# Four gated slots, gates and additions split by tile, and part of a modulation on TensorE between mixers and FFNs

## The chip, the cores and the metric

One core of one Trainium2 chip. The time is that of one launch in device microseconds, the median of several runs.

## What is computed

Two blocks of two layers each over one sequence of 256 tokens and width 1024, all in float32. In the first block every sublayer is a sandwich: the input is normed, scaled and shifted by a modulation of `c`; the output is normed again, gated and added.

```
def sandwich(x, mod, g_pre, g_post, fn):
    shift, scale, gate = mod
    h = rms_norm(x, g_pre) * (1.0 + scale[:, None]) + shift[:, None]
    return x + gate[:, None] * rms_norm(fn(h), g_post)
```

`mod` is `silu(c) @ ada_w + ada_b`, split in three. Sublayers in order: hybrid mixer (pool and a gated recurrence), SwiGLU (ffn0), dilated attention (qkv, att_out), SwiGLU (ffn1). The second block has plain pre-norms: mixer (even_in, even_out), MLP, axial attention (odd_in, odd_out), MLP.

## The kernel before

Everything is held as two tiles of 128 tokens in `x[:, tt, :]`. Weights come in loads of 1 MB through six raw slots (SyncE's queue); each load is two halves, and of every half ScalarE makes a high part (`whi`, line 513) and VectorE the low part (`wlo`, line 1210). TensorE multiplies high by high, high by low and low by high (`three`), so a product is three matmuls. Four halves of `whi` and `wlo` exist, and a split waits until TensorE is done with the half four before. TensorE's program order is written out by hand; engines meet by counting semaphores only.

Between two sublayers lies a seam, numbered j = 1 to 7 (line 2118 `turn(j)`). At seams 1 to 4 the output of the sublayer stands in four PSUM banks, `ps[:, 4 + i, :]`, i = 0 to 3: tile `i // 2`, half `i % 2` of the columns. What happens there:

- ScalarE, `norms(j)` (line 590): squares of y by bank with a running sum (`square_y`), the root of each tile (`root_y`, Ln and Exp), squares of the new x (`square_x`) and their roots (`root_x`).
- VectorE, `renew(j, bank)` (line 1327): y times gate (`gate_y`, line 1303) into `xn_of(p)[1]`, which has two slots of 512 columns, so the third and the fourth gate wait for the additions that read the first two; the addition to x once the root is there (`update_x`, line 1311); the small sums ahead of a root (`mean_y`, `mean_x`); x times its root (`scaled_x`, line 1324), tile 0 in one piece, tile 1 in two; and between them `mod_cols` (lines 1256 to 1258), which waits for `cols_sum` and makes the scale and shift columns out of PSUM.
- TensorE: column sums over partitions of a modulation (`sum_cols`, 16 matmuls with one column), dummies (`keep_warm`, into a bank that nobody reads), 16 transposes of the scaled x (`turn`, line 2126).
- then `pre(j)`: ScalarE and VectorE turn each of the eight transposed chunks k into a shifted float32 copy, a high part `hhi` and a low part `hlo` (line 1371); TensorE's first product of the next layer waits for `hlo` of each k (`turned_in`). With 2 x 128 output columns per half (`up`), a chunk k is worth 6 matmuls.

The modulation itself is worked out on VectorE beside other work: `ada_item` (lines 1220, 1223) multiplies one of eight chunks of a block of `ada_w` (512 columns) by a column of silu(c) and adds to `acc_a` or `acc_b`; Pool's queue loads the halves of a block (`ada_blocks`, line 439), each when `ada_step` says that the half in the same slot is used. Gate rows are summed over partitions by matmuls of `ones` (`sum_gates`), then `gate_add` and `gate_gain` on VectorE (lines 1267, 1273). The blocks 6 to 13 are worked out inside ffn0.

## Time and profile before

| what | us |
|---|---|
| median of 3 runs (1340.04 to 1345.56) | 1343.15 |
| the profiled execution, own time | 1342.11 |
| its span | 1340.2 |
| TensorE busy, share of the span | 1324.5, 99% |
| VectorE busy | 870.3, 65% |
| ScalarE busy | 721.7, 54% |
| mean granted clock of TensorE | 0.991 |

In the profile, engines are PE (TensorE), PEld (its weight loads), DVE (VectorE), ACT (ScalarE), POOL and SP (the queues). A busy TensorE may be at work on dummies or at half clock, so its share alone does not tell what a seam costs. Matmuls of float32 operands are two records each, transposes one.

### The profile page before, as it was taken

What the parts mean: (1) busy time and instruction counts of PE and PEld (TensorE: products, weight loads), DVE (VectorE), ACT (ScalarE), POOL (GpSimd) and SP (SyncE); (2) the same over time, 40 slices, a digit from 0 to 9 for tenths busy, and PEclk for the clock granted to TensorE, in tenths of its full rate; (3) what the DMA queues carried; (4) which work ended last, traced back from release to release, by engine and by line L of the source; (5) the groups of instructions that cost most, each with busy time, mean ns of one, the idle gap of its engine ahead of it and who ended that gap; (6) DMA issues with size and microseconds to landing.
All of it is one profiled execution on the core that took longest, in us unless ns stands there. A gap on an engine that the chain in (4) does not pass through costs nothing.

```text
span 1340.2 us, 22440 instructions
## 1 busy us (share of the span) xinstructions
PE 1324.5 (99%) x8876; PEld 1197.7 (89%) x8876; DVE 870.3 (65%) x1140; ACT 721.7 (54%) x1070; POOL 49.9 (4%) x76
## 2 busy tenths in 40 slices
PE   8999999999999999999999999999999999999999
PEld 7998899999899779999999899889999888899997
DVE  6889888885898566555565675565555577655554
ACT  3666644444644556444466763555555666655553
POOL 0100000000111000000001000000000000000000
PEclk8999999999899999999999999999999999999999
DMA  9978789985699624555537444455555552355540
GB/s 353 388 267 278 268 282 316 311 297 185 234 358 353 198 59 146 188 186 187 188 140 232 155 140 144 129 169 191 188 190 188 171 168 95 126 189 189 188 156 32
DMA packets 147362, 275.54 MB, mean 206 GB/s; under 512 B 4728, under 2 KB 85392, under 8 KB 147161
## 3 DMA queue, kind: packets, MB, share of 16 engines
q1 hardware_dynamic: 132176, 220.21, 48.7%
q0 software_dynamic: 13872, 52.05, 11.5%
q10 hardware_dynamic: 1240, 2.26, 0.5%
q8 instruction: 51, 0.84, 0.3%
q14 instruction: 23, 0.18, 0.0%
HBM read 273.40 MB, written 1.10 MB: 205 GB/s over the span
## 4 chain that ended last, share of the span: by engine, by line
PE 86%; DVE 6%; DMA 4%; issue 2%; ACT 2%; SPq 0%; ACTq 0%; DVEq 0%
PE ps L1985 84%; DMA raw<-in_ada_w 2%; DMA ada_ring<-in_ada_w 2%; DVE acc_a L1223 2%; DVE wlo L1210 1%; PE ps L2126 1%; PE ps L2362 1%; DMA raw<-in_hyb_w_in 1%; ACT whi L513 0%; ACT xn L567 0%; DVE xn L1324 0%; PE ps L2470 0%; ACT small L574 0%; DVE x L1318 0%; PE ps L2663 0%
## 5 line engine op out<-in xcount | busy, mean ns | idle before, releaser
L1210 DVE TENSOR_TENSOR wlo<-raw,whi 128x1024 fp32r<-128x1024 f32 x400 | 485.5, 1224 | 356.0 <-ACT whi L513 354.5
L513 ACT CAST whi<-raw 128x1024 fp32r<-128x1024 f32 x400 | 417.6, 1051 | 472.8 <-PE ps L1985 456.7
L1985 PE MATMUL ps<-hhi,whi 128*128 128x256 f32 x1792 | 507.4, 283 | 2.9 <-DVE hlo L1371 2.4
L1985 PE MATMUL ps<-hhi,wlo 128*128 128x256 f32 x1792 | 500.7, 279 | 0.0
L1985 PE MATMUL ps<-hlo,whi 128*128 128x256 f32 x1792 | 499.9, 279 | 0.0
L1985 PEld LDWEIGHTS ps<-hhi,whi 128*128 128x128 f32 x1792 | 335.9, 187 | 9.1 <-issue 6.2
L1985 PEld LDWEIGHTS ps<-hlo,whi 128*128 128x128 f32 x1792 | 336.2, 188 | 4.7 <-issue 2.4
L1985 PEld LDWEIGHTS ps<-hhi,wlo 128*128 128x128 f32 x1792 | 336.5, 188 | 0.0
L1985 PE MATMUL ps<-whi,hidhi 128*128 128x512 f32 x432 | 170.3, 394 | 0.0
L1985 PE MATMUL ps<-wlo,hidhi 128*128 128x512 f32 x432 | 169.1, 392 | 0.0
L1985 PE MATMUL ps<-whi,hidlo 128*128 128x512 f32 x432 | 168.6, 390 | 0.0
L1985 PE MATMUL ps<-whi,hhi 128*128 128x512 f32 (+1 forms) x256 | 101.8, 398 | 2.0 <-ACT att1o L790 0.8
L1223 DVE SCALAR_TENSOR_TENSOR acc_a<-ada_ring,sc,acc_a 128x512 f32<-128x512 f32 (+1 forms) x126 | 94.7, 752 | 6.8 <-DMA ada_ring<-in_ada_w 2.6
L1985 PEld LDWEIGHTS ps<-whi,hidlo 128*128 128x128 f32 x432 | 81.1, 188 | 18.6
L1985 PE MATMUL ps<-wlo,hhi 128*128 128x512 f32 (+1 forms) x256 | 97.6, 381 | 0.0
L1985 PE MATMUL ps<-whi,hlo 128*128 128x512 f32 (+1 forms) x256 | 97.5, 381 | 0.0
L1985 PEld LDWEIGHTS ps<-whi,hidhi 128*128 128x128 f32 x432 | 81.1, 188 | 16.0 <-issue 0.2
L1985 PEld LDWEIGHTS ps<-wlo,hidhi 128*128 128x128 f32 x432 | 81.1, 188 | 15.4 <-issue 0.2
L1985 PEld LDWEIGHTS ps<-whi,hhi 128*128 128x128 f32 x256 | 48.3, 189 | 14.5 <-issue 3.9
L1985 PEld LDWEIGHTS ps<-wlo,hhi 128*128 128x128 f32 x256 | 48.2, 188 | 10.4 <-issue 1.4
L1985 PEld LDWEIGHTS ps<-whi,hlo 128*128 128x128 f32 x256 | 48.2, 188 | 10.3
L439 POOL DMA_DIRECT2D ada_ring<-in_ada_w x40 | 30.4, 760 | 307.9 <-DVE acc_a L1223 222.1
(238 smaller groups left out, 1156.6 us busy)
## 6 DMA issues: line engine op xcount, KB each, us to landing
raw<-in_ffn_w_in SPq DMA_DIRECT2D x44, 1024.0 KB, 6.4
ada_ring<-in_ada_w POOLq DMA_DIRECT2D x40, 1024.0 KB, 7.3
raw<-in_w_mlp_up SPq DMA_DIRECT2D x32, 1024.0 KB, 5.4
raw<-in_w_mlp_down SPq DMA_DIRECT2D x32, 1024.0 KB, 5.0
raw<-in_ffn_w_out SPq DMA_DIRECT2D x22, 1024.0 KB, 5.0
raw<-in_att_w_qkv SPq DMA_DIRECT2D x18, 1024.0 KB, 6.8
raw<-in_w_in_even SPq DMA_DIRECT2D x18, 1024.0 KB, 4.9
raw<-in_hyb_w_in SPq DMA_DIRECT2D x10, 1024.0 KB, 12.0
```

The lines of the kernel that those rows point to most:

```text
L439: pool.dma_start(ada_ring[:, kh, :, :], src).then_inc(ada_in[kh], 16)
L513: A.copy(whi[:, H % 4, :], raw[:, slot(n), h * HALF:(h + 1) * HALF]).then_inc(s["hi_ready"], 1)
L1210: V.tensor_tensor(wlo[:, H % 4, :], raw[:, slot(n), h * HALF:(h + 1) * HALF], whi[:, H % 4, :].bitcast(F32), ALU.subtract).then_inc(s["lo_ ...
L1223: ins = V.scalar_tensor_tensor(out=out, in0=ada_ring[:, kh, kk, :], scalar=sc[:, k:k + 1], in1=out, op0=ALU.mult, op1=ALU.add)
L1985: return pe.matmul(out, lhsT, rhs, start=first, stop=last, skip_group_check=True)
L2126: m = pe.transpose(turned_ps(j, k)[:, tt * P:(tt + 1) * P], xn[:, tt, k * P:(k + 1) * P], ident[:, :])
L2362: m = pe.transpose(dl_turned(p, i)[:, (j - j0) * P:(j - j0 + 1) * P], dl_block(p, j), ident[:, :])
```

## The change

Seams 1 to 4 (`POST`), ScalarE and VectorE: y times gate goes to four slots of 512 columns, in `xn_of(p)[0]`, and the squares' discarded outputs go to `xn_of(p)[1]`. Tile 0's additions come right behind tile 0's root; each gate and addition of tile 1 follow one another. The two squares of x's tile 0 become one over 1024 columns (`square_tile`), whose sum needs no `mean_x`; `root_tile` takes it directly. The scaling of tile 0 stands behind all additions and behind `mean_x` of tile 1.

Ahead of ffn0: items 6 and 7 of block 5 leave VectorE; TensorE does them as 8 matmuls of one column each, straight from the ring into the bank of the column sums, which then add to it. After the 2nd, 6th, 10th and 14th of the 16 sums stand two dummies each, and in front of the transposes one in place of seven. VectorE's splits of halves 28 and 29 move: one behind the scaling of tile 1, one into `pre(1)` behind k = 3.

Ahead of qkv: TensorE sums the second gate ahead of the last but one down product in place of the last; VectorE's `gate_add` moves into the last body of ffn0. Ahead of ffn1: four dummies in place of seven.

```diff
--- before.py
+++ after.py
@@ -258,6 +258,11 @@
+        POST = (1, 2, 3, 4)
+        def means_x(j, tt):
+            return 2 * j + tt + 1 - sum(i in POST for i in range(j + 1))
         def xn_of(j):
@@ -557,14 +562,26 @@
                 y_ready(act, p, i)
-                A.activation(xn_of(p)[0][:, i // 2, c], ps[:, 4 + i, :], ACT.Square,
+                A.activation(xn_of(p)[1][:, i % 2, :], ps[:, 4 + i, :], ACT.Square,
                              accum_out=stat[:, i:i + 1]).then_inc(s["ssq_y"], 1)
+            def square_tile(j):
+                act.wait_ge(s["x_ready"], 4 * (j - 1) + 2)
+                A.activation(xn_of(j - 1)[1][:, :, :].rearrange("p a b -> p (a b)"), x[:, 0, :], ACT.Square,
+                             accum_out=stat[:, 5:6]).then_inc(s["ssq_x"], 2)
+            def root_tile(j):
+                act.wait_ge(s["ssq_x"], 4 * j + 2)
+                root(small[:, 5, 3:4], stat[:, 5:6], eps[:, 0:1], "ssq_x", 4 * j + 2, "root_x")
...
                 act.wait_ge(s["x_ready"], 4 * (j - 1) + i + 1) if j else act.wait_ge(s["x_in"], 16)
-                A.activation(xn_of(j)[0][:, i // 2, c], x[:, i // 2, c], ACT.Square,
+                junk = xn_of(j)[1][:, i % 2, :] if j in POST else xn_of(j)[0][:, i // 2, c]
+                A.activation(junk, x[:, i // 2, c], ACT.Square,
                              accum_out=stat[:, 4 + i:5 + i]).then_inc(s["ssq_x"], 1)
@@ -585,20 +602,24 @@
                 root(small[:, 5, 3 + tt:4 + tt], stat[:, 5 + 2 * tt:6 + 2 * tt], small[:, 5, 7 + tt:8 + tt],
-                     "mean_x", 2 * j + tt + 1, "root_x")
+                     "mean_x", means_x(j, tt), "root_x")
...
-                if j in (1, 2, 3, 4):
+                if j in POST:
                     square_y(j - 1, 0)
...
                     square_y(j - 1, 2)
-                    square_x(j, 0)
                     square_y(j - 1, 3)
                     root_y(j - 1, 1)
-                else:
-                    square_x(j, 0)
+                    square_tile(j)
+                    root_tile(j)
+                    square_x(j, 2)
+                    square_x(j, 3)
+                    root_x(j, 1)
+                    return
+                square_x(j, 0)
                 square_x(j, 1)
@@ -1298,19 +1319,17 @@
                 dve.wait_ge(s["ssq_y"], 4 * p + i + 1)
-                if i >= 2:
-                    dve.wait_ge(s["x_ready"], 4 * p + i - 1)
-                V.tensor_tensor(xn_of(p)[1][:, i % 2, :], ps[:, 4 + i, :], gg[:, p % 2, cols_of(i)], ALU.mult) \
+                V.tensor_tensor(xn_of(p)[0][:, i // 2, cols_of(i)], ps[:, 4 + i, :], gg[:, p % 2, cols_of(i)], ALU.mult) \
                     .then_inc(s["y_gated"], 1)
-            def update_x(p, tt):
+            def update_x(p, i):
+                tt = i // 2
                 dve.wait_ge(s["root_y"], 2 * p + tt + 1)
-                dve.wait_ge(s["y_gated"], 4 * p + 2 * tt + 2)
-                for i in (2 * tt, 2 * tt + 1):
-                    V.scalar_tensor_tensor(out=x[:, tt, cols_of(i)], in0=xn_of(p)[1][:, i % 2, :],
-                                           scalar=r_y[:, tt:tt + 1], in1=x[:, tt, cols_of(i)], op0=ALU.mult,
-                                           op1=ALU.add).then_inc(s["x_ready"], 1)
+                dve.wait_ge(s["y_gated"], 4 * p + i + 1)
+                V.scalar_tensor_tensor(out=x[:, tt, cols_of(i)], in0=xn_of(p)[0][:, tt, cols_of(i)],
+                                       scalar=r_y[:, tt:tt + 1], in1=x[:, tt, cols_of(i)], op0=ALU.mult,
+                                       op1=ALU.add).then_inc(s["x_ready"], 1)
@@ -1327,25 +1346,28 @@
                 p = j - 1
-                if j in (1, 2, 3, 4):
+                if j in POST:
                     dve.wait_ge(s["gates_ready"], p + 1)
                     gate_y(p, 0)
+                    mean_y(p, 0)
                     gate_y(p, 1)
-                    mean_y(p, 0)
                     update_x(p, 0)
+                    update_x(p, 1)
+                    mean_y(p, 1)
                     gate_y(p, 2)
-                    mean_y(p, 1)
+                    update_x(p, 2)
                     gate_y(p, 3)
-                    mean_x(j, 0)
-                    update_x(p, 1)
-                elif j:
+                    update_x(p, 3)
+                    mean_x(j, 1)
+                    scaled_x(j, 0, 0, D)
+                else:
                     add_y(p, 0)
...
                     add_y(p, 3)
-                scaled_x(j, 0, 0, D)
-                mean_x(j, 1)
+                    scaled_x(j, 0, 0, D)
+                    mean_x(j, 1)
                 if bank is not None:
@@ -1371,6 +1393,8 @@
                             shifted(k + 3)
+                        if j == 1 and k == 3:
+                            split(2 * FIRST["hyb_out"] + 9)
                     else:
@@ -1395,6 +1419,8 @@
                     split_some(g, it, before)
+                    if modulations and isinstance(it, int) and g == NG1 - 1:
+                        gate_add(1, 2)
                     dve.wait_ge(s["hhid_hi"], G + g + 1 + 2 * it)
@@ -1551,14 +1577,14 @@
             split(2 * FIRST["hyb_out"] + 7)
-            ada_part(acc_a, 5, 512 * 5, 1)
+            for k in (4, 5):
+                ada_item(acc_a, 5, 512 * 5, k)
             mod_gate(0, 2)
-            for q in range(4, 6):
-                split(2 * FIRST["hyb_out"] + 4 + q)
             renew(1, 0)
+            split(2 * FIRST["hyb_out"] + 8)
             pre(1)
             swiglu(FIRST["ffn0"], 0, True)
-            mod_gate(1, 2)
+            gate_gain(1)
             renew(2, 3)
@@ -2098,10 +2124,12 @@
-            def sum_cols(acc, n, bank):
+            def sum_cols(acc, n, bank, first=True):
                 for i in range(16):
-                    m = mm(ps[:, bank, i:i + 1], acc[:, n + i * P:n + (i + 1) * P], ones[:, 0:1])
+                    m = mm(ps[:, bank, i:i + 1], acc[:, n + i * P:n + (i + 1) * P], ones[:, 0:1], first, True)
+                    if not first and i % 4 == 1:
+                        keep_warm(2, 1)
                 m.then_inc(s["cols_sum"], 1)
@@ -2131,13 +2159,17 @@
-                def body(g, it=0, first=False):
+                def body(g, it=0, first=False, sums=False):
...
                     up(H0 + 6 + 6 * g, it, b + 1)
+                    if sums:
+                        pe.wait_ge(s["hid_ready"], G + g + 1)
+                        pe.wait_ge(s["ada_step"], 8 * 14)
+                        sum_gates(acc_b, 0, 2)
                     pe.wait_ge(s["hhid_lo"], G + g + 1 + 2 * it)
@@ -2145,13 +2177,12 @@
                 body(1, 0)
-                with pe.Fori(1, (NG1 - 1) // 2) as i:
+                with pe.Fori(1, (NG1 - 1) // 2 - 1) as i:
                     body(0, i)
                     body(1, i)
+                body(NG1 - 3)
+                body(NG1 - 2, sums=call == 0)
                 pe.wait_ge(s["hhid_lo"], G + NG1)
-                if call == 0:
-                    pe.wait_ge(s["ada_step"], 8 * 14)
-                    sum_gates(acc_b, 0, 2)
                 last_down(H0 + 6 * NG1 - 2, hid_c(hidhi1, (NG1 - 1) % 2), hid_c(hidlo1, (NG1 - 1) % 2))
@@ -2308,9 +2339,16 @@
             out_proj("hyb_out", 2, hhi[:, 4:8, :], hlo[:, 4:8, :], 2, False, True)
-            pe.wait_ge(s["ada_step"], 8 * 6)
-            sum_cols(acc_a, 2 * 512, 0)
-            turn(1, 7)
+            pe.wait_ge(ada_in[1], 16 * 6)
+            for k in (6, 7):
+                if k == 6:
+                    pe.wait_ge(s["ada_step"], 8 * 6 - 2)
+                for i in range(4):
+                    m = mm(ps[:, 0, 12 + i:13 + i], ada_ring[:, 1, k - 4, i * P:(i + 1) * P], sc[:, k:k + 1],
+                           k == 6 and i == 0, False)
+                m.then_inc(s["ada_step"], 1)
+            sum_cols(acc_a, 2 * 512, 0, False)
+            turn(1, 1)
             swiglu(FIRST["ffn0"], 0, 1)
@@ -2421,7 +2459,7 @@
             sum_cols(acc_a, 0, 0)
-            turn(3, 7)
+            turn(3, 4)
             swiglu(FIRST["ffn1"], 1, 3)

```

## Rows read from the trace of the kernel before

**Rows 1.** Page, part 1: busy us, share of the span, instructions.

```profile
PE 1324.5 (99%) x8876; PEld 1197.7 (89%) x8876; DVE 870.3 (65%) x1140; ACT 721.7 (54%) x1070; POOL 49.9 (4%) x76
```

**Rows 2.** The chain that ended last: start us, us, what.

```profile
154.84 192.61 PE ps L1985 x1358
...
699.60 30.86 PE ps L1985 x246
```

**Rows 3.** Timeline, first seam, all engines: start, us, engine, line, out<-in, count, [idle].

```profile
141.80 2.35 DVE L1210 TENSOR_TENSOR wlo<-raw,whi 128x1024 fp32r<-128x1024 f32 x2
...
143.28 3.64 PE L1985 MATMUL ps<-ones,acc_a 128*128 128x1 f32 x32
...
144.32 0.37 SPq L366 DMA_DIRECT2D raw<-in_ffn_w_in  x1
...
146.78 3.33 PE L1985 MATMUL ps<-ident 128*128 128x128 f32 x14
...
151.03 0.16 DVE L1256 TENSOR_TENSOR shcol<-ps,cols 128x8 f32<-128x8 f32 x1
...
151.11 2.55 PE L2126 MATMUL ps<-ident,xn 128*128 128x128 f32 x16 [1.00 <-DVE xn L1324]
...
151.85 0.88 DVE L1324 TENSOR_SCALAR xn<-x,small 128x256 f32<-128x256 f32 x2 [0.38 <-ACT small L576]
...
153.21 0.56 ACT L620 ACTIVATE h<-ps,shcol,scol 128x256 f32<-128x256 f32 x1 [1.47 <-PE ps L2126]
...
156.28 0.85 DVE L1371 TENSOR_TENSOR hlo<-h,hhi 128x256 fp32r<-128x256 f32 x2
```

**Rows 4.** Stretches: length, busy (count) by engine, granted clock (PEclk), DMA share, GB/s.

```profile
30.70:34.10 3.40, 3.40 (x32) 3.40 (x32) 1.12 (x4) 1.04 (x1) 1.65 (x2) 1.00 1.05 386
34.10:37.50 3.40, 3.40 (x15) 3.17 (x15) 3.09 (x6) 2.70 (x5) 0.00 (x0) 0.50 1.05 391
143.28:146.75 3.47, 3.47 (x33) 3.47 (x32) 2.81 (x6) 1.07 (x4) 0.00 (x0) 1.00 1.03 387
146.75:150.20 3.45, 3.36 (x16) 3.06 (x15) 3.37 (x8) 3.16 (x11) 0.00 (x0) 0.51 1.04 378
344.70:348.10 3.40, 3.40 (x12) 2.21 (x12) 2.96 (x9) 2.64 (x10) 1.28 (x2) 0.50 0.16 58
348.10:351.50 3.40, 3.40 (x14) 2.89 (x14) 1.47 (x4) 1.60 (x4) 0.77 (x1) 0.50 0.88 266
351.50:352.00 0.50, 0.50 (x3) 0.25 (x2) 0.50 (x2) 0.50 (x2) 0.00 (x0) 0.94 0.99 385
501.70:505.10 3.40, 3.40 (x18) 3.20 (x17) 2.90 (x9) 2.22 (x8) 0.00 (x0) 0.51 0.00 0
```

**Rows 5.** Timeline, second seam.

```profile
345.39 2.05 PE L1985 MATMUL ps<-acc_a,ones 128*128 128x512 f32 x2
...
346.05 0.75 DVE L1324 TENSOR_SCALAR xn<-x,small 128x1024 f32<-128x1024 f32 x1
...
347.24 3.62 PE L2126 MATMUL ps<-ident,xn 128*128 128x128 f32 x16
```

**Rows 6.** Timeline, third seam.

```profile
500.90 2.58 PE L1985 MATMUL ps<-ident 128*128 128x128 f32 x14
...
503.39 2.81 PE L2126 MATMUL ps<-ident,xn 128*128 128x128 f32 x16
```

**Rows 7.** Timeline, fourth seam.

```profile
692.39 4.40 PE L1985 MATMUL ps<-ident 128*128 128x128 f32 x38
...
693.39 0.58 ACT L560 ACTIVATE xn<-ps 128x512 f32<-128x512 f32 x1
...
697.02 2.47 PE L2126 MATMUL ps<-ident,xn 128*128 128x128 f32 x16 [0.23 <-DVE xn L1324]
```

**Rows 8.** Timeline of Pool and of VectorE in ffn0.

```profile
139.78 0.75 POOL L439 DMA_DIRECT2D ada_ring<-in_ada_w  x1 [4.54 <-DVE acc_a L1223]
...
180.00 3.11 DVE L1223 SCALAR_TENSOR_TENSOR acc_b<-ada_ring,sc,acc_b 128x512 f32<-128x512 f32 x4
```

## Prediction, made before the change was run

> **What bounds the kernel now.** The page first: TensorE is busy for 99% of the span [rows 1]. So the only time that an edit between two layers can win is the time in which TensorE waits or does work that is no product of the reference, and whatever it adds to TensorE's own stream is paid in full unless it fills such a gap. The chain that ended last shows where the gaps lie: 1358 matmuls in one piece from 154.84 us, another piece from 699.60 us, and small pieces of ScalarE and VectorE only between them [rows 2]. The change touches four of these seams: before ffn0 (about 143 to 155 us), before qkv (341 to 352), before ffn1 (497 to 507) and before even_in (692 to 700). I then read each seam in the timeline, with the granted clock beside it.
>
> First seam [rows 3]: the last product of out_proj ends at 143.28; 16 column sums follow (32 records, 3.5 us to the next start, so 0.22 us each), then 7 dummies that take 3.33 us. VectorE has scaled tile 0 only at 151.1 (TensorE idle for 1.00 us before it), the second tile at 151.85, the first shifted tile comes at 153.21 and the first product at 154.84. Here the norm decides, because VectorE is still splitting weights until 144.15. The clock beside it [rows 4]: full through the column sums, 0.51 from 146.75 to 150.20. Second seam [rows 5]: tile 0 is scaled at 346.05 + 0.75 = 346.8, but TensorE is busy with half of a gate sum until 347.44 and its transposes go on until 350.86, at a clock of 0.50 throughout [rows 4]. There TensorE's own stream decides, the norm does not. Third seam [rows 6]: dummies until about 503.2, transposes from 503.39, nearly gapless, clock 0.51 [rows 4]. Fourth [rows 7]: the transposes start at 697.02, when tile 0 is scaled, after TensorE has stood waiting for that; the norm decides.
>
> **The change, part by part.**
>
> *Own slots for gated y, new order of gates and additions, one square over tile 0.* No gate has to wait for an addition any more, so the third and fourth square of y on ScalarE come as soon as their bank is full. At the fourth seam the dummies start at 692.39, so the last bank is full at about 692.6, and its square runs at 693.39 [rows 7], 0.8 us late. From there ScalarE's order is as before (root of y, square of x's first tile, its root, two squares, the last root), except that one square of 1024 columns stands for one of 512. One of 512 takes 0.58 [rows 7]; the wide one costs between 0 and 0.58 more, I take 0.45. So the last root comes 0.8 - 0.45 = 0.35 earlier at best. Against it: the scaling of tile 0 now stands behind the additions of tile 1 and behind mean_x of tile 1, which needs the square after the wide one. Tile 0 is thus scaled when it is now, within 0.1, and the first transposed columns, which are what even_in's first product waits for, come no sooner. Gain at the fourth seam: 0 to 0.3, I take 0.1. At the second the transposes start behind the gate sum either way: 0. At the third, tile 0 is scaled when it is now, tile 1 some 0.3 sooner, but the transposes there run at half clock and end when they end now: 0.
>
> *First seam, work taken from VectorE.* Two of its modulation items and two weight splits (2.35 us [rows 3]) leave the stretch ahead of the norm. VectorE's own chain then ends some 3.5 us sooner: tile 1 could be scaled near 148.3 instead of 151.85. What is late next is TensorE. Its stream after 143.28 is now 8 single-column matmuls for the two items, 16 for the sums, 8 dummies among these and one in front of the transposes. At full clock: 24 x 0.22 + 9 x 0.23 = 7.35 us (a dummy is two records, and 38 of them took 4.40 us at full clock, so 0.23 each [rows 7]). The sums are complete at 150.4, where they are complete at 146.9 now. And VectorE waits for just that: mod_cols stands in its queue ahead of the scaling of tile 1, so both scalings of tile 1 and all after them are queued behind the column sums. From the end of that wait the present rows give the rest: mod_cols at 151.03, tile 1 at 151.85, shifted tile at 153.21, product at 154.84, so 3.8 us [rows 3], 3.95 with the hand-over. First product at 150.4 + 3.95 = 154.35: 0.5 us sooner, if the clock holds.
>
> *Does it hold?* The row shows it at 1.00 through the present sums and 0.51 from 146.75 [rows 4]. The dummies come after the tenth single-column matmul, so what TensorE does up to 146.75 is nearly what it does now: I take it that the clock falls there again. Where the start of the kernel alternates single-column matmuls with a few dummies (30.7 to 34.1) the clock was 1.00 and was 0.50 right after [rows 4], so the mixture is no proof against a fall. At 146.75 a full-clock remainder of 3.65 us is left. A low stretch of 3.4 us as at this seam now does 1.7 us of it: sums complete at 146.75 + 3.4 + 1.95 = 152.1, first product 156.05, **1.2 us later** than now. No fall is the lower end (-0.5), a stretch twice as long, as from 344.7 to 351.5 [rows 4], the upper: 146.75 + 6.8 + 0.25 = 153.8, product 157.75, +2.9. I take the middle one, nearest in place.
>
> *The moved splits.* The first of the two comes behind the scalings: ready before the first product in each case; 0. The second now stands in pre(1) after the fourth low part. The low parts of k = 3 and 4 run at 156.28 to 157.13 [rows 3]; the split (1.22 us, half of the 2.35) pushes the fifth to 158.35, usable at 158.5. TensorE reaches k = 4 after 24 matmuls; at 0.125 us each (30.86 us for 246 [rows 2]) that is 157.85. It waits 0.65 us; bounds 0 and 1.22. The rest follows without a gap. I take **+0.7**.
>
> *What else is queued.* Pool's load of the next modulation half waits for items which TensorE now makes: it goes out near 145 (143.28 + 8 x 0.22) instead of 139.78, with a gain row behind it; its data are used at 180.00 [rows 8]: 0. SyncE's load at 144.32 [rows 3] waits for the second moved split, so near 158 to 160; its slot is used by the fourth group of splits after that, about 20 us on: 0, and 5 us at worst if it is late. The gate sum ahead of ffn0's last products is moved, not removed: 0. gate_add inside the last body delays the low half of the hidden tile by 1.22 us, beside the whole down product of the group before, after which it is wanted: 0. Pulling the gates off the second seam frees VectorE there, where TensorE decides: 0.
>
> *Three dummies fewer at the third seam.* Transposes start when tile 0 is scaled, not when dummies end: 0 if the clock returns about 505, as now. Dummies and transposes stand together in that low stretch [rows 4, 6]; with fewer dummies it may return later. Half a microsecond of products at half clock costs 0.25; I take +0.2, with 2.2 as the upper end (products from 507.4 on at half clock for about 4.4 us).
>
> Whether transposes alone bring the clock back is what that rests on. The second seam shows it: from 347.24 there are only 16 transposes and one half gate sum, and the granted clock is 0.94 in the half microsecond after 351.50 [rows 4, 5]. The Trainium skill (TensorE: Matmul & The Clock Gate, "Part 4: PE-mode transpose") says that full clock does not engage for transposes, as they do not count as busy in the same way. By that rule the third seam would end on the upper value (+2.2 in place of +0.2). The trace disagrees with the rule, though not conclusively, because the gate sum stands in the same stretch.
>
> **Sum.** First seam +1.2 + 0.7, second 0, third +0.2, fourth -0.1: **+2.0 us** on the profiled execution, whose time is 1342.11 (span 1340.2 and 1.9 around it): 1344.1. The median of the three runs is 1343.15, 1.0 higher, and I forecast the change's median there: **1345.2 us**. A measurement of this kernel can tell about 0.5% from no change, 6.7 us; every case below lies within that.
>
> **The rivals.**
> - *The clock stays low for two such stretches at the first seam* (slower): +2.9 + 0.7 + 0.1 = +3.7, 1346.9. Place: the mixed column sums; price: half clock until 153.6; it decides once the dummies among single-column matmuls are too thin to bring the clock back. For it: the row at 30.7 and 34.1. Against it: 7 dummies in a row did bring it back by 150.2.
> - *The clock never falls at the first seam*: -0.5 + 0.7 + 0.1 = +0.3, 1343.4.
> - *Clock low into ffn1* (slower, place third seam): transposes do not raise it; forecast +2.0: +4.0, 1347.2. With the first rival as well +5.7, 1348.8.
> - *The norms do gain* (faster): ScalarE's earlier roots reach the first product at the third and fourth seam (-0.3 each), clock full at the first (-0.5), the fifth low part is in time (0) and the transposes of the second seam start 0.8 sooner because the clock falls later there: -1.9, 1341.3. For it: VectorE is freed of 2.35 us and more. Against: the busy TensorE rows at seams two and three.
>
> **How the numbers follow.** Forecast 0.4, longer low stretch 0.2, no fall 0.15, low into ffn1 0.1, gain 0.15. The run-to-run spread is 1340.0 to 1345.6. The range runs from below the gain case to the two slower rivals together: 1340.3 to 1349.0. Over 0.5% faster (under 1336.4) would need a gain larger than all idle time at the four seams: 0.02. Over 0.5% slower (above 1349.9) needs both slow clocks and a late load: 0.05. Within: 0.93.
>
> **What the new profile would show.** Right: a continuous TensorE stream of about 9 us from 143.3, mod_cols behind its end, transposes with no wait for scaled tiles, a wait of TensorE for the low part of about 0.7 us some 3 us into ffn0, a first product near 156. Second seam unchanged, transposes gapless. Third: 4 dummies, then a gap of over 1 us ahead of the transposes. Wrong: tile 1's scaling ahead of the column sums' end, a first product before 154, or a load that is waited for in ffn0.

## The result and the profile after

The changed kernel takes 1347.54 us (median of 12 runs, 1342.97 to 1354.02) against 1344.05 us for the kernel before (12 runs beside it, 1340.03 to 1345.75): ratio 1.0029, 95% interval 1.0015 to 1.0042, so 2 to 6 us slower. It is small, and in these runs clear of the noise; when both were run again (experiment 1) the interval was 1.0000 to 1.0031. The profiled execution has 1348.38 us. The ratios below leave out one run, of experiment 8, that took 5630.88 us.

The page of the changed kernel (span; part 1, columns as in [rows 1]) shows nothing of where the time went: TensorE is busy for 99%, as before, only longer.

```profile
span 1346.6 us, 22425 instructions
...
PE 1330.7 (99%) x8890; PEld 1204.3 (89%) x8890; DVE 868.9 (65%) x1134; ACT 721.9 (54%) x1062; POOL 49.7 (4%) x76
```

The timeline of the first seam, the lines that answer to [rows 3] (start, us, engine, line, what; L2011 is a matmul, L2154 a transpose):

```profile
146.71 1.84 PE L2011 MATMUL ps<-sc,ada_ring 128*128 128x1 f32 x16
...
148.86 0.69 PE L2011 MATMUL ps<-ident 128*128 128x128 f32 x4
149.39 0.95 PE L2011 MATMUL ps<-ones,acc_a 128*128 128x1 f32 x8
...
152.14 1.20 PE L2011 MATMUL ps<-ident 128*128 128x128 f32 x4
...
153.13 1.71 PE L2011 MATMUL ps<-ones,acc_a 128*128 128x1 f32 x8
...
156.58 0.17 DVE L1277 TENSOR_TENSOR shcol<-ps,cols 128x8 f32<-128x8 f32 x1 [5.30 <-PE ps L2011]
...
156.97 3.62 PE L2154 MATMUL ps<-ident,xn 128*128 128x128 f32 x16
157.06 0.88 DVE L1343 TENSOR_SCALAR xn<-x,small 128x256 f32<-128x256 f32 x2
...
159.62 0.57 ACT L641 ACTIVATE h<-ps,shcol,scol 128x256 f32<-128x256 f32 x1 [7.90 <-PE ps L2154]
```

and of TensorE alone right behind it:

```profile
161.25 0.35 PE L2011 MATMUL ps<-hhi,whi 128*128 128x256 f32 x1 [0.66 <-DVE hlo L1393]
...
164.73 0.36 PE L2011 MATMUL ps<-hhi,whi 128*128 128x256 f32 x1 [0.40 <-DVE hlo L1393]
```

TensorE starts its single-column matmuls at 146.71 and goes on without a gap until the transposes at 156.97: 10.26 us, where the kernel before has 7.83 with a wait of 1.00 in it. Matmuls overlap at their ends, so what two dummies (four records) cost is the time from their start to the start of what follows: 0.53 us at full clock (148.86 to 149.39) and 0.99 at half (152.14 to 153.13). VectorE's mod_cols (156.58) sits behind the end of the sums, and the scaling of tile 1 (157.06) behind that. The first product comes at 161.25, 14.54 us after the first sum (11.56 before). The clock in the same stretch (columns as in [rows 4]):

```profile
146.71:150.67 3.96, 3.96 (x37) 3.96 (x36) 3.10 (x8) 3.57 (x11) 1.29 (x2) 1.00 1.05 342
150.67:154.08 3.41, 3.41 (x20) 3.41 (x19) 0.61 (x1) 0.99 (x4) 0.00 (x0) 0.53 0.98 367
154.08:157.50 3.42, 3.42 (x17) 3.42 (x18) 0.85 (x5) 0.00 (x0) 0.00 (x0) 0.50 0.28 110
157.50:160.92 3.42, 3.09 (x15) 2.69 (x13) 2.36 (x4) 1.30 (x4) 0.00 (x0) 0.50 0.00 0
160.92:162.00 1.08, 0.75 (x6) 0.78 (x7) 1.08 (x4) 1.08 (x4) 0.00 (x0) 0.90 0.00 0
```

The clock is full (2.4 GHz) until about 150.9 (the mean of 0.53 in the second row is 0.2 us at full and the rest at half) and low (1.2 GHz) to about 161.1 (the mean of 0.90 in the last row), 10.2 us in one piece, through the rest of the sums, the dummies and all transposes.

The second, third and fourth seam, the lines that answer to [rows 5], [rows 6] and [rows 7]:

```profile
352.49 2.06 PE L2011 MATMUL ps<-acc_a,ones 128*128 128x512 f32 x2
...
352.96 0.74 DVE L1343 TENSOR_SCALAR xn<-x,small 128x1024 f32<-128x1024 f32 x1
...
354.34 2.58 PE L2154 MATMUL ps<-ident,xn 128*128 128x128 f32 x16
```

```profile
508.23 2.05 PE L2011 MATMUL ps<-ident 128*128 128x128 f32 x8
...
510.07 3.21 PE L2154 MATMUL ps<-ident,xn 128*128 128x128 f32 x16
```

```profile
699.56 0.60 ACT L565 ACTIVATE h<-ps 128x512 f32<-128x512 f32 x1 [0.69 <-PE ps L2011]
...
703.99 2.23 PE L2154 MATMUL ps<-ident,xn 128*128 128x128 f32 x16 [0.22 <-DVE xn L1343]
```

At the second, tile 0 is scaled at 353.70 (352.96 + 0.74) and TensorE's gate sum still ends later. At the third, four dummies come and then the transposes, without a gap. At the fourth, the last bank's square stands at 699.56, 0.2 us behind the start of the dummies (699.36); before it was 1.0 behind. The piece that starts with even_in in the chain that ended last, as in [rows 2], is of the same length:

```profile
706.37 30.88 PE ps L2011 x246
```

The seams from all profiles of the study, read from the timelines, all in us. A seam is counted from its first sum (the first single-column matmul; at the fourth seam the first dummy) to the next first product; ffn0 from its first product to the second seam's first sum; "low" is how long the clock was at half in one piece at the first seam:

| version | first sum at | seam 1 | low | ffn0 | seam 2 | seam 3 | seam 4 |
|---|---|---|---|---|---|---|---|
| before, profile 1 | 143.28 | 11.56 | 3.4 | 186.75 | 9.98 | 9.96 | 7.21 |
| before, profile 2 | 143.62 | 12.21 | 6.8 | 186.75 | 9.24 | 11.49 | 7.21 |
| before, profile 3 | 147.07 | 12.37 | 6.8 | 186.75 | 10.06 | 9.87 | 7.21 |
| changed, profile 1 | 146.71 | 14.54 | 10.2 | 187.65 | 9.19 | 10.73 | 7.01 |
| changed, profile 2 | 146.13 | 14.88 | 10.2 | 187.66 | 10.38 | 10.46 | 7.00 |
| first-seam part alone | 145.76 | 15.36 | 10.2 | 187.62 | 9.59 | 10.02 | 7.20 |
| first-seam part undone | 144.08 | 11.31 | 3.4 | 186.75 | 9.20 | 10.45 | 7.00 |
| the same, 7 dummies at seam 3 | 146.28 | 11.03 | 3.4 | 186.76 | 9.20 | 11.51 | 7.00 |
| no dummies among the sums | 146.95 | 11.23 | 6.8 | 187.63 | 9.19 | 9.91 | 7.01 |
| dummies in a row | 145.88 | 13.71 | 6.8 | 187.65 | 9.19 | 9.91 | 7.01 |
| split ahead of the low parts | 146.22 | 15.09 | 10.2 | 186.92 | 10.11 | 9.65 | 7.00 |
| mod_cols last | 145.51 | 15.36 | 10.2 | 187.65 | 9.16 | 9.51 | 7.00 |
| splits moved otherwise (experiment 9) | 146.38 | 10.03 | 3.4 | 186.99 | 9.19 | 9.85 | 7.00 |
| the same, one dummy | 147.41 | 10.40 | 6.8 | 186.76 | 9.18 | 9.46 | 7.00 |

Changed against before, first profiles: 6.4 us of span. 3.43 of them lie ahead of the first seam, up to which TensorE's program is the same; seam 1 gives +2.98, ffn0 +0.90, seam 2 -0.79, seam 3 +0.77, seam 4 -0.20, and the other stretches together the rest, -0.7.

The low clock at the first seam goes with the dummies among the sums: 10.2 us in all five profiles that have them there, 3.4 or 6.8 in all nine that have not, the kernel before included.

### The profile page after: what moved, and what is told of

It reads as the page before. It is cut to its first block, busy times and chain, and to the rows that moved or that the text cites. A ratio compares the mean times of both kernels' runs of the same rounds, so it can differ in the third digit from the quotient of the medians.

```text
span 1346.6 us, 22425 instructions
## 1 busy us (share of the span) xinstructions
PE 1330.7 (99%) x8890; PEld 1204.3 (89%) x8890; DVE 868.9 (65%) x1134; ACT 721.9 (54%) x1062; POOL 49.7 (4%) x76
## 4 chain that ended last, share of the span: by engine, by line
PE 96%; ACT 1%; DVE 1%; DMA 1%; issue 1%; ACTq 0%
PE ps L2011 94%; PE ps L2154 1%; PE ps L2400 1%; DMA voh<-in_voh 1%; ACT whi L518 0%; PE ps L2508 0%; DVE xn L1343 0%; DVE x L1337 0%; PE ps L2701 0%; DVE hlo L1393 0%; ACT xn L584 0%; ACT h L641 0%; ACT small L591 0%; DVE hlo L1943 0%; ACT hhi L643 0%
## 5 line engine op out<-in xcount | busy, mean ns | idle before, releaser
L2011 PE MATMUL ps<-hhi,whi 128*128 128x256 f32 x1792 | 507.0, 283 | 3.0 <-DVE hlo L1393 2.4
L2011 PE MATMUL ps<-hhi,wlo 128*128 128x256 f32 x1792 | 500.6, 279 | 0.0
L2011 PE MATMUL ps<-hlo,whi 128*128 128x256 f32 x1792 | 500.0, 279 | 0.0
L2011 PEld LDWEIGHTS ps<-hhi,whi 128*128 128x128 f32 x1792 | 335.9, 187 | 10.0 <-issue 7.4
L2011 PEld LDWEIGHTS ps<-hlo,whi 128*128 128x128 f32 x1792 | 336.3, 188 | 4.4 <-issue 2.2
L2011 PEld LDWEIGHTS ps<-hhi,wlo 128*128 128x128 f32 x1792 | 336.4, 188 | 0.0
L2011 PE MATMUL ps<-whi,hidhi 128*128 128x512 f32 x432 | 170.2, 394 | 0.0
L2011 PE MATMUL ps<-wlo,hidhi 128*128 128x512 f32 x432 | 169.3, 392 | 0.0
L2011 PE MATMUL ps<-whi,hidlo 128*128 128x512 f32 x432 | 168.6, 390 | 0.0
L2011 PE MATMUL ps<-whi,hhi 128*128 128x512 f32 (+1 forms) x256 | 102.1, 399 | 2.0 <-ACT att1o L811 0.8
L2011 PE MATMUL ps<-wlo,hhi 128*128 128x512 f32 (+1 forms) x256 | 97.8, 382 | 0.0
L2011 PEld LDWEIGHTS ps<-whi,hidlo 128*128 128x128 f32 x432 | 81.1, 188 | 18.6
L2011 PE MATMUL ps<-whi,hlo 128*128 128x512 f32 (+1 forms) x256 | 97.6, 381 | 0.0
L2011 PEld LDWEIGHTS ps<-whi,hidhi 128*128 128x128 f32 x432 | 81.1, 188 | 16.1 <-issue 0.2
L2011 PEld LDWEIGHTS ps<-wlo,hidhi 128*128 128x128 f32 x432 | 81.1, 188 | 15.3 <-issue 0.2
L2011 PEld LDWEIGHTS ps<-whi,hhi 128*128 128x128 f32 x256 | 48.4, 189 | 14.5 <-issue 3.9
L2011 PEld LDWEIGHTS ps<-wlo,hhi 128*128 128x128 f32 x256 | 48.4, 189 | 10.4 <-issue 1.4
L2011 PEld LDWEIGHTS ps<-whi,hlo 128*128 128x128 f32 x256 | 48.4, 189 | 10.3
```

Source lines behind the costliest of these rows:

```text
L2011: return pe.matmul(out, lhsT, rhs, start=first, stop=last, skip_group_check=True)
```

## The experiments

Unless said otherwise an edit is made to the changed kernel.

**1. The changed kernel again** (no edit).

> The changed kernel once more. Theory (the time is lost at the first seam, in TensorE's longer stream and at half clock): from the first column sum to ffn0's first product 13 to 15 us, against 11.56 in the profile of the kernel before; from there to the second seam's sums about 0.7 to 0.9 us more than 186.75; median 2 to 5 us above the kernel before. Rival (the two profiles differ mostly by what happens ahead of the first seam, 3.4 us of their 6.4, by chance of that execution): the first sum comes near 143.3 again in this profile, and the median is within 1.5 us of the kernel before.

1347.59 us (12 runs), the kernel before beside it 1344.11 (35 runs); ratio 1.0015, interval 1.0000 to 1.0031. Seam 1 is 14.88, ffn0 187.66. The first sum is at 146.13, not 143.3. The theory's numbers hold for the seam and ffn0; where the late start comes from is experiment 5.

**2. The first-seam part alone, in the kernel before, and 3. that part undone, in the changed kernel.**

```diff
-            ada_part(acc_a, 5, 512 * 5, 1)
+            for k in (4, 5):
+                ada_item(acc_a, 5, 512 * 5, k)
             mod_gate(0, 2)
-            for q in range(4, 6):
-                split(2 * FIRST["hyb_out"] + 4 + q)
             renew(1, 0)
+            split(2 * FIRST["hyb_out"] + 8)
...
-            sum_cols(acc_a, 2 * 512, 0)
-            turn(1, 7)
...
+            sum_cols(acc_a, 2 * 512, 0, False)
+            turn(1, 1)
```

(the edit of 2, cut: left out are the split inside `pre(1)`, the 8 item matmuls and the dummies inside `sum_cols`; 3 is the inverse of the whole)

> The kernel before with only that part: two modulation items on TensorE, dummies among the sums, two splits moved. Theory: first seam 13 to 15 us, median 2 to 5 us above the kernel before, as the changed kernel. Rival: within 1.5 us of the kernel before.

> The changed kernel with only the part ahead of ffn0 undone: both modulation items and both splits back on VectorE ahead of the norm, 16 sums and seven dummies on TensorE. Theory (all of the loss is in that part; the new order of gates and additions gives 0 to 0.5 us): first seam 11.3 to 11.6 us, no wait for the fifth low part, median 0 to 1 us below the kernel before. Rival (the new order of the norms, or three dummies fewer at the third seam, is what costs): median stays 2 us or more above the kernel before, third seam 10.7 us again instead of 9.96.

Alone: 1348.24 us, ratio 1.0029 (1.0013 to 1.0045), seam 1 15.36 (a little above the 13 to 15 expected), ffn0 187.62: the whole loss. Undone: 1342.45 us, ratio 0.9994 (0.9977 to 1.0012), seam 1 11.31, ffn0 186.75: no loss left. Both ran beside the same runs of the kernel before as experiment 1. The theory stands: the loss is in the first-seam part, and the new order of the norms costs nothing that these runs show. The fourth seam tells what that order gives: 7.20 with the old order (alone), 7.00 with the new one (undone).

**4. Why the stream is long: no dummies among the sums, and all nine dummies in a row behind them.**

```diff
-                    if not first and i % 4 == 1:
-                        keep_warm(2, 1)
...
-            turn(1, 1)
+            turn(1, 9)
```

(the last two lines in the second version only)

> The changed kernel without the eight dummies among the column sums. Theory (the dummies cost their own length and do not keep the clock up): the stream from the first single-column matmul to the last shrinks from 10.3 us to 6 to 7.5 us and the first product of ffn0 comes 2 to 4 us sooner than in the changed kernel (10.5 to 12.5 us after the first sum); median 2 to 3 us below the changed kernel. Rival (the dummies do hold the clock up in most executions, and their lack is paid in transposes and first products at half clock): first product 13 us or more after the first sum, median same as or above the changed kernel.

> The changed kernel with all nine dummies in a row behind the sums, none among them: the same 33 pieces of work on TensorE, in another order. Theory A (what costs most is the mixture: it does not bring the clock back, a row of dummies does): low clock for 3.4 or 6.8 us instead of 10.2, first seam 12 to 13.5 us. Theory B (the length of the stream alone counts): 14.3 us or more, as with the dummies among the sums. Either way the column sums end sooner, so VectorE makes the scale and shift columns while the dummies run.

Without them: 1345.27 us, ratio 1.0010 (0.9997 to 1.0023). That is 2.3 us below the median of the changed kernel beside it, but the intervals of the two ratios (1.0010, and 1.0015 in experiment 1) overlap widely, so the total does not settle it; the seam does, at 11.23. TensorE's timeline without them:

```profile
146.95 1.84 PE L2011 MATMUL ps<-sc,ada_ring 128*128 128x1 f32 x16
148.65 4.83 PE L2011 MATMUL ps<-ones,acc_a 128*128 128x1 f32 x32
153.34 0.78 PE L2011 MATMUL ps<-ident 128*128 128x128 f32 x2
153.91 3.62 PE L2152 MATMUL ps<-ident,xn 128*128 128x128 f32 x16
```

The transposes start after 6.96 us, not 10.26. In a row: 1344.38 us, ratio 1.0013 (0.9996 to 1.0030), seam 1 13.71, between what the two theories gave (12 to 13.5, and 14.3 or more), nearer the first:

```profile
145.88 1.84 PE L2011 MATMUL ps<-sc,ada_ring 128*128 128x1 f32 x16
147.58 5.58 PE L2011 MATMUL ps<-ones,acc_a 128*128 128x1 f32 x32
153.02 3.65 PE L2011 MATMUL ps<-ident 128*128 128x128 f32 x18
156.50 1.91 PE L2152 MATMUL ps<-ident,xn 128*128 128x128 f32 x16
159.59 0.35 PE L2011 MATMUL ps<-hhi,whi 128*128 128x256 f32 x1 [1.18 <-DVE hlo L1393]
```

The 32 records of the sums take 5.58 us, partly at half clock; from 156.50 the transposes take 1.91, so the clock is back by then, and the scale and shift columns are long made. The clock is low for 6.8 us in both versions here, 10.2 in the changed kernel.

What the mixture costs can be added up from start to start. The eight dummies among the sums occupy 3.04 us (two pairs at 0.53, two at 0.99); the 16 sums between them take 0.27 us more than without them; together 3.3, which is all of the difference between 14.54 and 11.23, as from the first transpose to the first product both need 4.3. At full clock the eight dummies would take 2.1 us, so about two thirds of these 3.3 us are their bare length and one third is half clock. In a row, nine dummies and the sums take 10.62 us up to the transposes, no less than in the changed kernel, but the clock is back for these, and 3.09 us later the first product comes. That share of the order, 0.8 us, rests on one profile; like versions spread from 14.54 to 15.36.

The two items themselves cost the seam nothing: with them on TensorE and without the eight dummies it is 11.23, with them on VectorE and seven dummies in front of the transposes 11.31 (experiment 3). What the first version here keeps of the loss is the 0.9 us in ffn0.

**5. The kernel before, profiled twice more.**

> The kernel before, profiled once more. Theory (what happens ahead of the first seam differs between executions of the same code): the first column sum starts anywhere from 143 to 147 us; first seam 11.0 to 12 us, ffn0 186.75. Rival (the shift of the start belongs to the changed kernels): 143.3 again.

> The kernel before, profiled a third time. Two profiles of it have the first column sum at 143.28 and 143.62 us, nine of other versions with the same code up to there at 144.1 to 147.4. Theory (chance of the execution): 144 to 147 us is as likely as not. Rival (the later start belongs to the changed kernels in some way): 143.0 to 143.9 a third time. First seam 11.3 to 12.3 us, third 9.9 to 11.5 as in the first two.

The first sum is at 143.62 and 147.07. (The recorded text counts nine other profiles; there were eleven.) The first 44 us of the kernel before, in its first profile and in its third:

```profile
0.00:44.00 44.00, 39.95 (x235) 33.79 (x236) 31.80 (x60) 20.14 (x40) 2.80 (x7) 0.88 1.00 361
```

```profile
0.00:44.00 44.00, 38.50 (x218) 32.75 (x219) 28.84 (x53) 17.81 (x35) 2.79 (x7) 0.77 0.98 350
```

The granted clock is 0.88 in the one and 0.77 in the other, which is that of the changed kernel's profile too (0.77). Over all fourteen profiles the first sum comes earliest where the clock was low for the shortest time in the first 60 us: at 143.28, 143.62 and 144.08 with 10.2, 10.2 and 13.7 us of half clock, at 145.5 to 147.4 with 17.1 or 20.5. TensorE's program up to there is the same in all versions, and the kernel before has both the earliest start and one of the latest; so 3.4 of the 6.4 us between the first two profiles are an accident of execution. The seams of the kernel before vary as well: 11.56 to 12.37 at the first, where seven dummies in a row were followed by a full clock after 3.4 us in the first profile and only after 6.8 in the two others. In its second profile TensorE waits 2.06 us there and the transposes run at half clock:

```profile
147.11 2.34 PE L1985 MATMUL ps<-ident 128*128 128x128 f32 x14
151.50 3.67 PE L2126 MATMUL ps<-ident,xn 128*128 128x128 f32 x16 [2.06 <-DVE xn L1324]
```

**6. The moved split.**

```diff
             split(2 * FIRST["hyb_out"] + 8)
+            split(2 * FIRST["hyb_out"] + 9)
             pre(1)
```

(and the split inside `pre` removed)

> The changed kernel with the second moved split taken out of the eight low parts and put ahead of them. Theory (it alone makes TensorE wait for the fifth low part): no wait inside ffn0's first product, from first product to the second seam 186.75 us instead of 187.65; VectorE starts the shifted copies about 0.7 to 1.2 us later, so the first seam grows by 0.3 to 1.2 us and the sum is about even. Rival (the 0.9 us come from loads or modulation items that are late inside ffn0): 187.6 us still.

ffn0 is 186.92 instead of 187.65, and the wait for the fifth low part is gone; seam 1 is 15.09. VectorE's first shifted copy starts behind two splits at 160.19, 0.4 later than in the changed kernel (159.78):

```profile
157.91 2.35 DVE L1231 TENSOR_TENSOR wlo<-raw,whi 128x1024 fp32r<-128x1024 f32 x2
160.19 0.54 DVE L1383 TENSOR_SCALAR h<-ps,scol,shcol 128x256 f32<-128x256 f32 x1
```

1346.31 us, ratio 1.0013 (0.9999 to 1.0028): not to be told from the changed kernel. The wait is caused by the split. That it is paid again at the seam, as I expected, is not shown: from the first transpose to the first product it takes 4.28 us in both, and the low part that this product waits for starts 3.71 us after the first transpose in both (160.74 and 160.68); the late copy is over just in time. The longer seam lies ahead of the transposes (10.81 us against 10.26 and 10.61 in the changed kernel), where the clock fell sooner, 3.6 us after the first sum and not 4.2 or 3.8. Seam 1 and ffn0 together are 202.0, against 202.2 and 202.5.

**7. mod_cols behind the scaling of tile 1.**

```diff
-                if bank is not None:
+                if bank is not None and j != 1:
                     mod_cols(j, bank)
                 scaled_x(j, 1, 0, 256)
                 scaled_x(j, 1, 256, D)
+                if bank is not None and j == 1:
+                    mod_cols(j, bank)
```

> The changed kernel with the scale and shift columns of the first seam made behind the scaling of tile 1 instead of ahead of it. Theory (VectorE's queue holds the scaling of tile 1 behind the column sums, but TensorE's transposes cannot start before the sums end either): tile 1 scaled 4 us or more ahead of the end of the sums; first product 0.2 to 0.7 us sooner relative to the first transpose, no more. Rival (that wait is the whole of the loss): first seam back to 11.6 us.

```profile
150.55 0.88 DVE L1343 TENSOR_SCALAR xn<-x,small 128x256 f32<-128x256 f32 x2 [0.47 <-ACT small L593]
156.33 0.17 DVE L1277 TENSOR_TENSOR shcol<-ps,cols 128x8 f32<-128x8 f32 x1 [4.89 <-PE ps L2013]
```

Tile 1 is scaled 4.9 us before the sums end, and it helps by almost nothing: from the first transpose to the first product 4.15 us instead of 4.28, less than the 0.2 to 0.7 expected, and the version of experiment 2, without this edit, has 4.16. 1345.93 us, ratio 1.0013 (1.0001 to 1.0025). The queued wait that the prediction describes is real but hidden behind TensorE's own stream.

**8. Seven dummies at the third seam** (in the version of experiment 3, `turn(3, 7)` for `turn(3, 4)`).

> The changed kernel with the part ahead of ffn0 undone and seven dummies at the third seam instead of four: what is left of the change is the new order at the four seams and the moved gate sum. Theory (with four dummies the clock stays low longer at the third seam in some executions): third seam 9.9 to 10.0 us, against 10.45 to 10.7 in three of four profiles with four dummies; median at or up to 1 us below the version with four. Rival (the number of dummies changes nothing): third seam up to 10.7 us as well.

The third seam is 11.51, so the theory falls. With four dummies the seven profiles give 9.51 to 10.73 (mean 10.1), with seven 9.46 to 11.51 (mean 10.3). 1344.05 us, ratio 0.9989 (0.9974 to 1.0004). The number of dummies there decides nothing that these runs can tell. One cost lies outside the table: in the profile of the dummies in a row the clock was low for 10.2 us from 504.11, on into ffn1, and the stretch from there to the fourth seam took 187.20 us where twelve of the other thirteen profiles have 185.0. That is the 2.2 us of the prediction's rival "clock low into ffn1", seen in one of seven profiles with four dummies and in none of seven with seven.

**9. A version that uses what is left of the change.** Both items and the seven dummies as before; the new norms; one split behind the third gate and one behind the scaling of tile 1. (The diff is cut: the lines that put items and dummies back are those of experiment 3.)

```diff
                     gate_y(p, 2)
+                    if j == 1:
+                        split(2 * FIRST["hyb_out"] + 8)
                     update_x(p, 2)
...
             renew(1, 0)
-            split(2 * FIRST["hyb_out"] + 8)
+            split(2 * FIRST["hyb_out"] + 9)
             pre(1)
```

> A version for the sum of what was seen: new order of the norms kept, both modulation items on VectorE, 16 sums and seven dummies as before, the two splits placed in VectorE's gaps (one behind the third gate, one behind the scaling of tile 1), seven dummies at the third seam. Theory (VectorE's relief is worth something once TensorE's stream is short): scaling of tile 1 about 1.3 us sooner than in the kernel before, first seam 10.0 to 10.6 us instead of 11.56, ffn0 at 186.75; median 1 to 3 us below the kernel before. Rival (the seam is set by transposes at half clock, not by the norm): 11.3 us or more.

> The version with the splits in VectorE's gaps, with one dummy in place of seven behind the 16 sums of the first seam. Theory (with the norm ahead at 153.4 these dummies fill a gap and only serve the clock): transposes start as early as with seven or up to 0.2 us sooner; if the clock stays low without them, the transposes and the first products run at half clock and the first seam is 10.5 to 12.5 us instead of 10.03. Rival (dummies are useless there): 10.0 us or less.

```profile
146.38 3.63 PE L2010 MATMUL ps<-ones,acc_a 128*128 128x1 f32 x32
...
148.67 1.22 DVE L1231 TENSOR_TENSOR wlo<-raw,whi 128x1024 fp32r<-128x1024 f32 x1
...
149.87 3.22 PE L2010 MATMUL ps<-ident 128*128 128x128 f32 x14
...
152.88 2.36 PE L2153 MATMUL ps<-ident,xn 128*128 128x128 f32 x16
...
153.42 0.88 DVE L1343 TENSOR_SCALAR xn<-x,small 128x256 f32<-128x256 f32 x2 [0.36 <-ACT small L593]
154.22 1.22 DVE L1231 TENSOR_TENSOR wlo<-raw,whi 128x1024 fp32r<-128x1024 f32 x1
...
156.41 0.35 PE L2010 MATMUL ps<-hhi,whi 128*128 128x256 f32 x1 [1.18 <-DVE hlo L1395]
```

and of the version of experiment 8, which has the same norms and both splits ahead of them:

```profile
146.28 3.63 PE L2009 MATMUL ps<-ones,acc_a 128*128 128x1 f32 x32
...
154.32 0.88 DVE L1343 TENSOR_SCALAR xn<-x,small 128x256 f32<-128x256 f32 x2 [0.24 <-ACT small L593]
```

The second split stands where VectorE waited for the transposes. The first was meant for the wait for the second root of y, which is 0.69 us long in the changed kernel; here that root is ready at 148.77, the gate ends at 148.75, and the split pushes the next addition to 149.80, so nearly all of it is paid. Tile 1 is scaled 7.0 us after the first sum, 8.0 in the version of experiment 8 and 8.57 in the kernel before; seam 1 is 10.03, against 11.03 and 11.56 to 12.37. Read this way the 1.0 us between 11.03 and 10.03 are the second split's; a version with that one alone moved was not run. The rest goes with the new order and with the clock, low for 3.4 us here as in the version of experiment 8. 1342.18 us against 1344.31 for the kernel before beside it: ratio 0.9987, interval 0.9975 to 0.9999, just faster than that kernel, and below the changed one. The version of experiment 8 has 0.9989 beside the same runs, so the totals do not show what the splits give; only the seam does. With one dummy (`turn(1, 1)`) TensorE stands waiting for the scaled tile, and the transposes run at half clock:

```profile
153.49 3.67 PE L2153 MATMUL ps<-ident,xn 128*128 128x128 f32 x16 [1.59 <-DVE xn L1343]
```

Seam 1 is 10.40, which is between the two expectations, and the time 1341.52 us, ratio 0.9995 (0.9979 to 1.0012): one dummy and seven are not told apart.

## Why the prediction was right, and where it was not

The forecast was 1345.2 us, +2.0; measured are 1347.5, +3.5 (by the ratio +3.9, and by that of experiment 1 +2.0). It lies within the range and has the sign that the sum gave. The terms of the sum, first profile against first profile, come to +3.7; of these -0.79 at the second and +0.77 at the third seam are the clock's chance, see below, and it is luck that they cancel.

*TensorE's stream as what is late next*: right. It runs on without a gap, and the norm, ready for tile 0 at 151.3 (150.54 + 0.74), waits for it. Experiments 2 and 3 put the whole loss in the first-seam part.

*The clock*: this is the term that was mis-sized. The prediction took a low stretch of 3.4 us as in the kernel before, worth 1.7 us, and counted only the sums at half speed. The stretch was 10.2 us. Of the 10.26 us up to the transposes 6.1 ran at half clock, worth 3.0 us; at full clock the stream would have been 7.2, so its length (7.35) was sized rightly. The sums were complete 9.9 us after TensorE's first single-column matmul (forecast 8.8), and from there to the first product it took 4.7 us, not 3.95, with all transposes at half clock. 14.5 us for the seam is the figure of the first rival (157.75 - 143.28 = 14.47), but by two misses that cancel: it had two low stretches of 3.4 and not three, the sums complete after 10.5 us and the rest at 3.95. The middle value was called "nearest in place"; the row at the kernel's start, where the same mixture was followed by a low clock, was the nearer one in kind. And the 3.4 us were read from one profile: the two later ones of the kernel before have 6.8. That the clock fell about where it does in the kernel before was right (4.2 us after the first sum, 3.5 before).

*The wait for the fifth low part*: forecast 0.65 to 0.7. At the fifth part it is 0.65; over ffn0 the loss is 0.90, of which 0.73 goes when the split is moved (experiment 6). VectorE's split stands between the fourth and the fifth,

```profile
162.69 0.42 DVE L1393 TENSOR_TENSOR hlo<-h,hhi 128x256 fp32r<-128x256 f32 x1
163.02 1.23 DVE L1231 TENSOR_TENSOR wlo<-raw,whi 128x1024 fp32r<-128x1024 f32 x1
164.16 0.43 DVE L1393 TENSOR_TENSOR hlo<-h,hhi 128x256 fp32r<-128x256 f32 x1
```

and TensorE starts its fifth chunk at 164.73 where 24 matmuls of 0.118 from 161.25 end at 164.08.

*mod_cols in VectorE's queue*: the queue was seen right, but the path behind the sums was not. The prediction led its 3.95 us through mod_cols and the scaling of tile 1; at half clock it runs through the transposes, which reach tile 1 only after it is scaled, and taking mod_cols out of the way changes 4.28 to 4.15 (experiment 7). *The second seam* at zero: near. It follows the clock more than the order. With a low stretch of 3.4 us there it is 9.16 to 9.20 in eight profiles of the new order, 9.24 and 9.59 in two of the old; with 6.8 us 10.11 and 10.38 in the new, 9.98 and 10.06 in the old. The -0.79 of the first profiles is 3.4 against 6.8 us of low clock. *Third* +0.2: 10.73 and 10.46 in the two profiles of the changed kernel against 9.96, 11.49 and 9.87, nothing over all of them (experiment 8). The gap of over 1 us ahead of the transposes, which was to show there, did not: the clock fell 2.3 us after the first sum (4.3 before), and the sums took 4.6 us instead of 3.5. In the profiles of experiment 4, where it was full through the sums, TensorE waits 0.96. *Fourth* -0.1: -0.20 in every profile of the new order. *Pool's and SyncE's late loads* at zero: near: with both still late and the split out of the way ffn0 is 186.92, 0.17 above the kernel before (experiment 6).

*Whether transposes alone raise the clock*: in the row 157.50 to 160.92 TensorE does nothing but transposes (156.97 + 3.62 = 160.59), and the clock is back at about 161.1. In the version with one dummy (experiment 9) TensorE is idle from 151.90 to 153.49, then does only the transposes, and the clock is back at 157.5. And once it is back, transposes run at it: 16 in 1.91 us in the second version of experiment 4, against 3.62. The Trainium skill (TensorE: Matmul & The Clock Gate, "Part 4: PE-mode transpose") says, of a case in bf16, that full clock does not engage for them. The traces disagree for these float32 transposes, now without another matmul in the stretch. That is no promise that it returns in time: in the profile with the dummies in a row it stayed low behind the third seam's transposes, on into ffn1 (told under experiment 8).

What stays open: why the stretch between seams 2 and 3 is 143.1 to 143.3 us in three profiles and 145.5 to 145.9 in the others, of whatever version; where the last 0.2 us of ffn0 come from; and whether the order of the dummies alone, at equal number, is worth the 0.8 us of its one profile.

## What to carry to other kernels

When an engine is busy for 99% of the span, work that is moved onto it is only free where it takes the place of filling or of a wait; add up its whole new stream first, at half clock as well. Here the 1.7 us of the two items cost the seam nothing, as dummies had stood there; the eight dummies put among the sums cost 3. Among single-column matmuls they did not hold the clock in any of five profiles, and each cost its length, doubled once the clock was low. Look also for gaps in the relieved engine's own queue, and check in the new profile that the gap is still there: of two splits the one put where VectorE waited for transposes is what the 1.0 us gained at the seam go with, and the one put at a wait that the version no longer had was paid almost in full.

## What the runs showed that was not expected

A low clock can last three times as long as in the profile that one reads: 3.4 or 6.8 us at the same seam of the same kernel, and 10.2 us of the changed one. Two profiles of the same code differ by up to 3.8 us ahead of 147 us (143.28 and 147.07), with a granted clock of 0.88 and 0.77 over the first 44 us; more than the whole effect of this change, so a difference of two spans is to be split by stage before anything is read from it.
